# Reading the moving columns of the main fp32r matmuls forwards instead of backwards

## The reference

```python
def ffn(h, w_up, w_down):
    a = jax.nn.relu(h @ w_up)
    return (a * a) @ w_down

xp = xp + rmsnorm(op, g_mix_post[i])
xp = xp + rmsnorm(ffn(rmsnorm(xp, g_ffn_pre[i]), w_ffn_up[i], w_ffn_down[i]), g_ffn_post[i])
```

## Time and profile before

| | |
|---|---|
| median of 3 runs | 2187.09 us (2186.81 to 2188.61) |
| profiled execution: its own time | 2186.82 us |
| profiled execution: span in the trace | 2185.1 us |
| TensorE matmuls busy | 2159.0 us, 99% of the span |
| VectorE busy | 1226.2 us, 56% |
| ScalarE busy | 992.0 us, 45% |
| GpSimd busy | 202.1 us, 9% |
| HBM traffic | 386 MB, 177 GB/s over the span |

### The profile page before, as it was taken

How to read it: one execution, slowest core, us unless ns; L and a number is a source line. 1 busy time by engine, 2 the same in 40 slices (tenths; PEclk the granted TensorE clock), 3 DMA queues, 4 the chain that set the end, 5 groups by cost and what they waited for, 6 DMA issues and landing times.

```text
span 2185.1 us, 43155 instructions
## 1 busy us (share of the span) xinstructions
PE 2159.0 (99%) x17793; PEld 2138.3 (98%) x17793; DVE 1226.2 (56%) x1329; ACT 992.0 (45%) x1239; POOL 202.1 (9%) x154
## 2 busy tenths in 40 slices
PE   7999999999999999999999999999999999999998
PEld 7999999999999999999999999999999999999998
DVE  6566756654554555455575675575455445545553
ACT  5545544543443344344454564454344334434543
POOL 3002211000000000011213201200000000001112
PEclk9999999999999999999999999999999999999999
DMA  7853454656565755565545555555565656556551
GB/s 222 230 191 129 152 183 142 193 177 188 177 189 175 226 176 188 177 185 181 179 149 176 173 172 175 173 157 189 175 188 176 187 178 185 180 182 184 181 183 61
DMA packets 380643, 386.91 MB, mean 177 GB/s; under 512 B 6804, under 2 KB 378316, under 8 KB 380430
## 3 DMA queue, kind: packets, MB, share of 16 engines
q1 hardware_dynamic: 374530, 380.02, 56.1%
q10 hardware_dynamic: 6036, 5.80, 0.8%
HBM read 380.10 MB, written 5.71 MB: 177 GB/s over the span
## 4 chain that ended last, share of the span: by engine, by line
PE 93%; DVE 5%; ACT 1%; DMA 0%; issue 0%; POOL 0%; DVEq 0%; SPq 0%; ACTq 0%; POOLq 0%
PE ps L1462 30%; PE ps L1464 30%; PE ps L1463 30%; DVE hlo L1045 1%; DVE wlo L1020 1%; DVE wlo L1012 1%; DVE x L1074 1%; DVE y L1069 0%; PE ps L1769 0%; PE ps L1840 0%; PE ps L1680 0%; PE ps L1666 0%; DMA region<-in_x_prompt_dram 0%; ACT hhi L640 0%; DVE region L1445 0%
## 5 line engine op out<-in xcount | busy, mean ns | idle before, releaser
L1012 DVE TENSOR_TENSOR wlo<-raw,whi 128x1024 fp32r<-128x1024 f32 x688 | 864.9, 1260 | 761.0 <-ACT whi L602 760.4
L602 ACT ACTIVATE whi<-raw 128x1024 fp32r<-128x1024 f32 x688 | 727.5, 1060 | 1017.0 <-PE ps L1464 1012.7
L1462 PE MATMUL ps<-hhi,whi 128*128 128x264 f32 x2944 | 842.5, 286 | 5.3 <-DVE hlo L1045 3.3
L1463 PE MATMUL ps<-hlo,whi 128*128 128x264 f32 x2944 | 835.2, 284 | 0.0
L1464 PE MATMUL ps<-hhi,wlo 128*128 128x264 f32 x2944 | 835.1, 284 | 0.0
L1462 PE MATMUL ps<-ahi,whi 128*128 128x264 f32 x2560 | 726.6, 284 | 0.0
L1464 PE MATMUL ps<-ahi,wlo 128*128 128x264 f32 x2560 | 724.6, 283 | 0.0
L1463 PE MATMUL ps<-alo,whi 128*128 128x264 f32 x2560 | 724.5, 283 | 0.0
L1462 PEld LDWEIGHTS ps<-hhi,whi 128*128 128x128 f32 x2944 | 555.4, 189 | 12.0 <-issue 6.4
L1464 PEld LDWEIGHTS ps<-hhi,wlo 128*128 128x128 f32 x2944 | 555.4, 189 | 0.0
L1463 PEld LDWEIGHTS ps<-hlo,whi 128*128 128x128 f32 x2944 | 555.2, 189 | 0.1
(11 more groups left out here) (219 smaller groups left out, 996.8 us busy)
## 6 DMA issues: line engine op xcount, KB each, us to landing
raw<-in_w_ffn_up_dram SPq DMA_DIRECT2D x128, 1024.0 KB, 5.6
raw<-in_w_ffn_down_dram SPq DMA_DIRECT2D x128, 1024.0 KB, 5.3
raw<-in_w_in_even_dram SPq DMA_DIRECT2D x36, 1024.0 KB, 5.1
raw<-in_w_in_cmlp_dram SPq DMA_DIRECT2D x32, 1024.0 KB, 5.5
raw<-in_w_out_even_dram SPq DMA_DIRECT2D x16, 1024.0 KB, 5.3
raw<-in_w_out_cmlp_dram SPq DMA_DIRECT2D x16, 1024.0 KB, 5.3
region<-in_x_prompt_dram SPq DMA_DIRECT2D x4, 512.0 KB, 8.0
out_y_prompt_dram<-region SPq DMA_DIRECT2D x8, 256.0 KB
```

The lines of the kernel that those rows point to most:

```text
L602: act.activation(whi[:, QK * q:QK * q + QK, :], raw[:, 2 * par + q // 2, k, :], ACT.Copy).then_inc(w_hi_ready, 1)
L1012: dve.tensor_tensor(wlo[:, QK * q:QK * q + QK, :], raw[:, 2 * par + q // 2, k, :], whi[:, QK * q:QK * q + QK, :].bitcast(F32), ALU.subtrac ...
L1462: pe.matmul(out, whi[:, k, cols], hi[:, k, ::-1], start=(k == 0), stop=False)
L1463: pe.matmul(out, whi[:, k, cols], lo[:, k, ::-1], start=False, stop=False)
```

## The change

Every main matmul, the six product lines and the warm-up line, reads its 264 moving columns from first to last and writes its 264 PSUM columns from first to last. Since both sides were reversed before and neither is now, each token's result lands in the same PSUM column as before. The weight operands, the allocation of `whi` and `wlo` with rows of 264 elements, the order of all instructions on all engines, the semaphores and the transfers are the same in both programs.

```diff
@@ quarter
-                        out = ps[:, 2 * par + j, 0:T][:, ::-1]
-                        pe.matmul(out, whi[:, k, cols], hi[:, k, ::-1], start=(k == 0), stop=False)
-                        pe.matmul(out, whi[:, k, cols], lo[:, k, ::-1], start=False, stop=False)
-                        mm = pe.matmul(out, wlo[:, k, cols], hi[:, k, ::-1], start=False, stop=(k == CH - 1))
+                        out = ps[:, 2 * par + j, 0:T]
+                        pe.matmul(out, whi[:, k, cols], hi[:, k, :], start=(k == 0), stop=False)
+                        pe.matmul(out, whi[:, k, cols], lo[:, k, :], start=False, stop=False)
+                        mm = pe.matmul(out, wlo[:, k, cols], hi[:, k, :], start=False, stop=(k == CH - 1))
@@ wave
                 for i in range(warm):
-                    pe.matmul(ps[:, i % 2, 0:T][:, ::-1], whi[:, i % QK, 0:P], ahi[:, i % QK, ::-1],
+                    pe.matmul(ps[:, i % 2, 0:T], whi[:, i % QK, 0:P], ahi[:, i % QK, :],
                               start=True, stop=True)
...
-                            out = ps[:, 2 * par + j, 0:T][:, ::-1]
-                            pe.matmul(out, whi[:, wk, cols], hi[:, k, ::-1], start=(k == 0), stop=False)
-                            pe.matmul(out, whi[:, wk, cols], lo[:, k, ::-1], start=False, stop=False)
-                            mm = pe.matmul(out, wlo[:, wk, cols], hi[:, k, ::-1], start=False, stop=(k == CH - 1))
+                            out = ps[:, 2 * par + j, 0:T]
+                            pe.matmul(out, whi[:, wk, cols], hi[:, k, :], start=(k == 0), stop=False)
+                            pe.matmul(out, whi[:, wk, cols], lo[:, k, :], start=False, stop=False)
+                            mm = pe.matmul(out, wlo[:, wk, cols], hi[:, k, :], start=False, stop=(k == CH - 1))
```

## The result

The changed kernel takes 2213.73 us (median of 4 runs, 2212.29 to 2215.01) against 2187.07 us (4 runs, 2186.81 to 2188.61): a ratio of 1.0119, 95% interval 1.0107 to 1.0132. It is slower by 26.7 us. The forecast was +56 us: the right side, but twice too large. The profiled execution after the change took 2215.01 us with a span of 2213.3, 28.2 us more than the span before.

What follows compares the result with a forecast made beforehand. TensorE's own pace was taken as the bound, 17088 main matmuls at 0.120 us. The one term, +3.3 ns x 17088 = +56 us on 2186.8, gave 2243 us, with a range of 2184 to 2290 us.

Steps and rivals of the forecast that it cites:

- TensorE's own pace is the bound, the feeders have slack, one term counts in full: Main matmuls: 0.120 us each, ScalarE and VectorE wait; 17088 x (new step - 0.120 us) is the whole change.
- The step is not a property of the instruction alone; the two reads from SBUF are coupled, and the other direction may settle elsewhere: Main matmuls: moving read and weight load beside it settle at 0.120 us backwards, possibly at another step forwards; slower, chance 0.52.
- The value I take, 0.1233 us: Forward step of the main matmuls, the mean over a stretch of settled and unsettled steps: +3.3 ns each, +56 us.
- The coupling term: Extra step of each of 17088 main matmuls from moving read meeting weight load: +3.3 ns, +56 us.
- the three steps: Three main matmuls in a row after a change from other work, read as 0.127 us each instead of 0.12.
- my stretch: Main matmul starts from 1018.66 to 1019.40 in the earlier trace, six steps, read as a mean of 0.1233 us.
- Durations rise from 0.28 to 0.29 with the step: Sign to look for: main matmul durations go from 0.28 to 0.29 us if the slower forecast is right.
- A step that alternates between matmuls of one triple would speak for the coupling: Sign in the main matmuls: uneven steps within a triple favour coupling; equal steps favour the stream alone.
- No difference: Rival: both directions of the main matmuls' walk touch the same columns and memory lines, so 2187 us; chance 0.33.
- Faster: walking backwards is what costs the 8 ns: Rival: each of 17088 streams drops from 0.120 to 0.112 us, -137 us, 2050 us; chance 0.15.
- The row against the coupling: A main matmul with no load behind it until 0.66 us later still lasts 0.28 us, so part of 8 ns is the stream's.

Runs made afterwards that it cites:

- read_back_write_fwd: Kernel before the change, with main matmuls still reading moving columns last to first but writing PSUM first to last: 2186.70 us.
- fwd_off32: Changed kernel with the used elements of whi and wlo moved by 32 bytes inside their rows: 2187.16 us; timed again, median 2187.73 us.
- back_off16: Kernel before the change (backward walk), with whi and wlo moved by 16 bytes inside their rows: 2220.70 us.
- fwd_wlo_off32: Changed kernel (forward walk) with only wlo moved by 32 bytes inside its rows, whi left in place: 2189.25 us.
- back_n200: Kernel before the change, with all main matmuls walking backwards over 200 of the 264 columns: 2053.23 us.
- fwd_n200: The same 200 of 264 columns in all main matmuls, walked forwards as in the changed kernel: 2053.26 us.
- fwd_n256: All main matmuls walk forwards, as in the changed kernel, over 256 of the 264 columns: 2159.18 us.
- fwd_off16: Changed kernel (forward walk) with whi and wlo moved by 16 bytes inside their rows: 2211.66 us.

## Why the prediction was right or wrong

- *TensorE's own pace is the bound, the feeders have slack, one term counts in full*: right. The term by the measured step, 28.4 us, is the 28.2 us of span, and the idle time of ScalarE grew by 27.2.
- *The step is not a property of the instruction alone; the two reads from SBUF are coupled, and the other direction may settle elsewhere*: right. The PSUM write is out (read_back_write_fwd), the stream alone is out (fwd_off32 with the same stream at 120.14), and the place of the load is in. The side, slower and not faster, came from no mechanism: the prediction says that nothing in the trace places the forward walk. At 16 bytes the same change goes the other way, so the right side was in part luck.
- *The value I take, 0.1233 us*: this is the step of the prediction that failed. The coupling term was sized at 3.3 ns and measured 1.66. Two things were wrong in it. The first is the source: I had taken the mean of a stretch of settled and unsettled matmuls as if the forward walk would alternate between these states. It settles instead, into a fixed cycle in which short steps (115.8, 116.7) pay back part of the long ones (up to 132.5). A transient of three matmuls gives the kind of disturbance, not the size of a settled state; the settled states measured with 264 columns lie anywhere from 120.14 to 122.49 ns. The second is the reading of the earlier trace rows: the starts are printed to 0.01 us, too coarse for differences of a few nanoseconds. In the whole nanoseconds of the trace the three steps are 123, 127 and 124, the next is 118, and the mean of my stretch is (1019.397 - 1018.665) / 6 = 0.1220 us. That would have given +2 ns and 2221 us, close to the result, but by luck, since the mean over only the three is 124.7 ns.
- *Durations rise from 0.28 to 0.29 with the step*: only for some of the matmuls. The mean rose by 0.6 ns.
- *"A step that alternates between matmuls of one triple would speak for the coupling"*: it does. The triples of back_off16 are 124.2, 123.3, 122.5 and 121.7, 124.2, 118.3 ns, and in the changed kernel the steps differ over 24 matmuls.
- *No difference*: fell. A move of one weight tile by 32 bytes, with nothing else changed (fwd_wlo_off32), is worth 1.66 ns a matmul. The Trainium skill, "SBUF — State Buffer", section "Who interferes with whom", calls TensorE's two read ports independent; if that means that the place of the weights cannot slow the stream, the runs do not agree.
- *Faster: walking backwards is what costs the 8 ns*: fell, since neither direction goes under 120.14 ns at any offset tried. Its argument that a cost of going backwards would not be 3% of a column's time has a slip: 8 ns over 264 columns are 0.03 ns a column, 7% of the 0.42 ns that it takes. The Trainium skill, "TensorE: Matmul & The Clock Gate", section "Back-to-back issue gap", gives N / 2.4 + 2.5 ns for an isolated matmul; that would be 112.5 ns for 264 columns and 109.2 for 256 (estimates from that page), while the best steps measured are 120.14 and 117.92. The prediction leaves out that the same section keeps a stream of weight loads and matmuls apart from this formula, so it was no forecast for this loop.
- *The row against the coupling*, 0.28 us with no load beside it: the duration is no measure of the stream. With 64 columns fewer, 27 ns of stream by the estimate above, it fell by only 8 ns, from 283 to 275 (back_n200).

What stays open: which part of the addresses decides, what in the entry picks the state, why the cycle has 6, 24, 48 or 108 matmuls, and why a state costs what it costs. Offsets other than 0, 16, 24 and 32 bytes were not tried, nor was a kernel in which both operands keep their place from `k` to `k`.

## What to carry to other kernels

Where fp32r matmuls of some 256 columns each bring their own weight load, the distance of their starts can depend by 2% on where the weight rows lie in SBUF and which way the moving tile is read (120.14 to 122.49 ns here). Read it from start to start over a few hundred matmuls, never from a few starts printed to 0.01 us, in more than one stretch, and look whether the steps are even. Before crediting an access direction or a row spacing with a gain, move one operand by 16 or 32 bytes and measure again: here that undid the loss, and made the good direction the worse one. Moving the weights inside rows that have spare elements takes no instruction and no memory, so it is easy to try.

## What the runs showed of the hardware

- With 200 columns and a weight load of 128 columns for each fp32r matmul the step is 111.67 ns in both directions, at a granted clock of 1.00 in the stretch measured (back_n200, fwd_n200). That the load sets it is argued.
- With 256 and 264 columns the best step is 117.92 and 120.14 ns, 11 and 10 ns over the columns at 2.4 GHz: 8 columns less bring 2.2 ns, not 3.3.
- The step depends on where the weights lie and on the direction of the moving read together: backwards 120.14, 122.36 and 120.14 ns at 0, 16 and 32 bytes, forwards 121.80, 121.62 and 120.14.
- The same loop with the same addresses can run in two settled states in one execution, 117.92 and 119.03 ns (fwd_n256) or 121.62 and 122.36 ns (fwd_off16). The longest unbroken runs, 5183 matmuls each, stayed in one.
- The direction of a PSUM write of 264 fp32 columns makes no difference: 120.14 ns in either with the backward read, 121.80 and 121.81 with the forward one.
